# A hybrid decoder layer: the second half of the tokens takes the indexer's first query tile into the keys' loop over contraction tiles

## What is computed

```python
h = rms_norm(x, mix_norm[l])
z = h @ w_in
(aq, ak, av, iq, ik, iw, pin, gu, gv, sq, sk, sv, gl) = jnp.split(z, _split_points(), axis=-1)
...
head_scores = jax.nn.relu(jnp.einsum('bthd,bsd->bths', qib, k_idx_f))
idx_score = jnp.einsum('bth,bths->bts', wb, head_scores)
...
x = x + hybrid_mixer(h, ...)
x = x + swiglu_ffn(rms_norm(x, ffn_norm[l]), ...)
```

## Time and profile before

| | |
|---|---|
| median of 3 runs | 755.93 us (755.53 to 756.05) |
| the profiled execution's own time | 755.91 us |
| its span (what the profile covers) | 754.0 us |
| PE busy | 748.6 us, 99% of the span |
| DVE / ACT / POOL busy | 590.8 / 405.2 / 105.0 us |
| moved by DMA | 89.55 MB |

### The profile page before, as it was taken

One profiled execution on the slowest core, in us unless ns is written; L12 is line 12 of the kernel. 1 busy time (PEld: TensorE's weight loads), 2 busy tenths in 40 slices (PEclk: granted clock), 3 DMA queues, 4 the chain that ended last, 5 costly groups with the idle time before them and its releaser, 6 DMA issues.

```text
span 754.0 us, 11466 instructions
## 1 busy us (share of the span) xinstructions
PE 748.6 (99%) x4494; PEld 660.8 (88%) x4494; DVE 590.8 (78%) x816; ACT 405.2 (54%) x629; POOL 105.0 (14%) x130
## 2 busy tenths in 40 slices
PE   8999999999999999999999999999999999999998
PEld 8988888988888888778888899999889999999886
DVE  5645998878788976425988989889989888888991
ACT  6644545456663654435349655556544556566430
POOL 7100050457303121211231000000000000000000
PEclk9999999999999999999999999999999999999999
DMA  8381213221133222317226725335073333338102
GB/s 274 104 245 42 75 57 113 65 104 57 57 112 99 70 76 92 112 57 278 85 82 176 189 112 157 114 110 210 4 254 108 113 111 111 113 113 321 70 29 83
DMA packets 67877, 89.55 MB, mean 119 GB/s; under 512 B 3108, under 2 KB 52592, under 8 KB 67696
## 3 DMA queue, kind: packets, MB, share of 16 engines
q1 hardware_dynamic: 66224, 85.60, 34.7%
q0 software_dynamic: 1456, 3.09, 2.0%
q10 hardware_dynamic: 144, 0.13, 0.1%
HBM read 81.99 MB, written 4.19 MB: 114 GB/s over the span
## 4 chain that ended last, share of the span: by engine, by line
PE 97%; POOL 1%; issue 1%; DVE 1%; ACT 0%; DVEq 0%; POOLq 0%
PE bank L2358 14%; PE bank L2360 14%; PE bank L2359 14%; PE bank L2784 8%; PE bank L2785 8%; PE bank L2786 8%; PE bank L2846 5%; PE bank L2850 5%; PE bank L2848 5%; PE bank L2725 2%; PE bank L2724 2%; PE bank L2723 2%; PE bank L2755 1%; PE bank L2754 1%; PE bank L2756 1%
## 5 line engine op out<-in xcount | busy, mean ns | idle before, releaser
L2358 PE MATMUL bank<-h_hi,w_hi 128*128 128x512 f32 (+1 forms) x352 | 134.7, 383 | 0.3 <-DVE w_lo L1600 0.3
L2360 PE MATMUL bank<-h_hi,w_lo 128*128 128x512 f32 (+1 forms) x352 | 133.8, 380 | 0.0
L2359 PE MATMUL bank<-h_lo,w_hi 128*128 128x512 f32 (+1 forms) x352 | 133.6, 380 | 0.0
L2784 PE MATMUL bank<-t_hi,w_hi 128*128 128x256 f32 x320 | 88.4, 276 | 0.0
L2786 PE MATMUL bank<-t_hi,w_lo 128*128 128x256 f32 x320 | 88.4, 276 | 0.0
L2785 PE MATMUL bank<-t_lo,w_hi 128*128 128x256 f32 x320 | 88.4, 276 | 0.0
L1529 DVE TENSOR_TENSOR w_lo<-raw,w_hi 128x2048 fp32r<-128x2048 f32 x27 | 64.2, 2379 | 24.1 <-ACT w_hi L918 17.0
L2358 PEld LDWEIGHTS bank<-h_hi,w_hi 128*128 128x128 f32 x352 | 66.2, 188 | 12.7 <-ACT w_hi L981 0.5
L2360 PEld LDWEIGHTS bank<-h_hi,w_lo 128*128 128x128 f32 x352 | 66.2, 188 | 12.6
L2359 PEld LDWEIGHTS bank<-h_lo,w_hi 128*128 128x128 f32 x352 | 66.2, 188 | 12.2
L2785 PE MATMUL bank<-f_lo,w_hi 128*128 128x256 f32 x240 | 66.3, 276 | 0.0
(11 more groups left out here) (374 smaller groups left out, 1858.1 us busy)
## 6 DMA issues: line engine op xcount, KB each, us to landing
raw<-in_w_in_dram SPq DMA_DIRECT2D x26, 1024.0 KB, 5.2
raw<-in_w_ffn_up_dram SPq DMA_DIRECT2D x11, 1024.0 KB, 5.1
raw<-in_w_ffn_gate_dram SPq DMA_DIRECT2D x10, 1024.0 KB, 5.2
raw<-in_w_ffn_down_dram SPq DMA_DIRECT2D x7, 1024.0 KB, 5.1
raw<-in_w_branch_dram SPq DMA_DIRECT2D x4, 1024.0 KB, 4.8
b<-in_w_ffn_down_dram SPq DMA_DIRECT2D x4, 1024.0 KB, 7.0
x_sb<-in_x_dram SPq DMA_DIRECT2D x6, 512.0 KB, 4.7
o<-in_w_out_dram SPq DMA_DIRECT2D x3, 1024.0 KB, 8.5
```

Of the source, the lines that this page charges most:

```text
L2358: mm(dst, l_hi, r_hi, start=start, stop=False)
L2359: mm(dst, l_hi, r_lo, start=False, stop=False)
L2360: return mm(dst, l_lo, r_hi, start=False, stop=stop)
L2784: mm(dst, l_hi, r_hi, start=begin and k == 0, stop=False, skip_group_check=True)
```

## The change

The two or three matmuls of a contraction tile become a helper, `queries(cols, j, k)`. In the second half of the tokens the queries' tile j = 0 is taken into the keys' loop: for each k the two matmuls of the keys are followed by the three of query tile 0. `filled` is still raised in the order keys, j = 0, j = 1. The loop over query tiles behind it starts at j = 1 in the second half. The first half is as before.

```diff
+            def queries(cols, j, k):
+
+                w = slice(w_at(1) + k * CW + j * P, w_at(1) + k * CW + (j + 1) * P)
+                return three(bank[1 + j][:, cols], w_hi[:, w], w_lo[:, w], h_hi[:, k, cols], h_lo[:, k, cols],
+                             k == 0, k == KT - 1)
+
...
                         mm(bank[0][:, cols], w, h_hi[:, k, cols], start=k == 0, stop=False)
                         last = mm(bank[0][:, cols], w, h_lo[:, k, cols], start=False, stop=k == KT - 1)
-                    if half:
-                        last.then_inc(filled, 1)
-                    for j in range(MT):
+                        if half:
+                            if k == KT - 1:
+                                last.then_inc(filled, 1)
+                            last = queries(cols, 0, k)
+                            if k == KT - 1:
+                                last.then_inc(filled, 1)
+                    for j in range(half, MT):
...
-                            w = slice(w_at(1) + k * CW + j * P, w_at(1) + k * CW + (j + 1) * P)
-                            last = three(bank[1 + j][:, cols], w_hi[:, w], w_lo[:, w], h_hi[:, k, cols], h_lo[:, k, cols],
-                                         k == 0, k == KT - 1)
-
+                            last = queries(cols, j, k)
```

## The result

| | before | changed |
|---|---|---|
| median | 755.99 us (755.53 to 756.57, 6 runs) | 758.78 us (757.59 to 759.13, 6 runs) |
| ratio | | 1.003, 95% interval 1.0017 to 1.0044 |
| profiled execution: time, span | 755.91, 754.0 us | 758.81, 756.8 us |
| mean granted clock, by execution | | 0.997 to 0.998 in five, 1.0 in the one of 757.59 |

The change costs 2.79 us, 0.37%, where 0.97 over the median of the three runs shown before was forecast (756.9, range to 757.6). It is slower by more than the interval, and outside the range.

What follows compares the result with a forecast made beforehand. PE, busy 99%, was taken as the bound. The loop's 0.36 us gain is spent waiting for the late `ikw`; chunk 2 starts at 32.20 instead of 31.21, so 755.91 + 0.99 = 756.90 us, range 755.9 to 757.6.

Steps and rivals of the forecast that it cites:

- Part 1: Keys' loop and query tiles on PE: pacing by `h_lo` goes, chunk 1 ends at 29.97, PE 0.36 us ahead.
- a change of bank: Interleaved loop: bank 0 to 1 taken as 0 extra; rival of 0.08 us each, 757.86 us, chance 0.07.
- Part 2: Later transposes for k = 6 and 7: `h_hi` of k = 7 0.64 us late, nothing by themselves.
- Part 3: Later keys' `filled`: ACT's chunk 3 1.72 us late, `ikw` ends 31.77, PE waits 1.37, chunk 2 starts 32.20.
- the DMAs of `iq_lo`: POOL's four DMAs, behind chunk 2: about 1.3 us later, landing by 41.0 before the reader at 43.2, costing nothing.
- Its own wait, `w_lo` of chunk 3, ends at 28.90 + 2.28 = 31.18 and is hidden by that of `ikw`: Start of chunk 2 on PE: its wait for `w_lo` ends at 31.18, hidden by the wait for `ikw`.
- The 0.33 us from L2617 to chunk 2: From the first transposes of `ikw` to chunk 2's first matmul: 0.33 us, so chunk 2 starts at 32.20.
- the gain of 0.36 us: Gain from the keys' loop, expected to be spent waiting for `ikw`; rival that it stays, 755.55 us, chance 0.06.
- the clock: Rival: behind PE's new 1.37 us pause the clock falls to 1.2 GHz; 2 us so spent gives 758.9; chance 0.03.
- The loop, the second place that the prediction named: Clock rival's other place: the interleaved loop, 5.3 us long, falling there would give up to 762 us.
- The passage on cycling through banks: Skill's rule cited against the change: bank cycling with pauses between groups; by it the clock would fall in the loop.

Runs made afterwards that it cites:

- x2: Kernel before, only the keys' `filled` raised later, by the last matmul of k = 5 of query tile 0, second half; 757.54 us.
- x3: Changed kernel with the keys' weights in a place of their own, so `w_hi` of chunk 3 need not wait for `filled`; 756.65 us, ratio 1.001.
- x9: x3 with the query groups of k = 0, 1, 2 all behind the keys of k = 2, transposes at their old moments; 755.93 us, ratio 1.0.
- x5: Changed kernel with 10 filler identity transposes before the wait for `ikw` and 2 behind the transposes of `ikw`; 757.23 us.
- x8: x4 with `iq_lo` of tile 0 ahead of `ikw` on DVE, transposes of `ikw` between chunk 2's first two tiles; 756.29 us, ratio 0.9994.
- x6: Changed kernel with the wait for `ikw` and its four transposes moved from ahead of chunk 2 to between its first two tiles; 759.54 us.
- x4: Kernel before with only the first group of three query matmuls taken ahead of the keys' matmuls of k = 5; 756.01 us, ratio 1.0001.
- x7: Kernel before, only the keys' `filled` raised later, by the last matmul of k = 6 of query tile 0; 759.22 us.
- x1: Changed kernel with 18 filler identity transposes before the wait for `ikw` and 4 behind the transposes of `ikw`; 758.44 us.

## Why the prediction was wrong

**Right.** Part 1: the loop steps at 0.12, ends at 29.98 (forecast 29.97), 0.35 us ahead, and a change of bank costs nothing. Part 2 (the transposes between k = 0 and 1 are those for k = 6, between k = 1 and 2 those for k = 7; no others stand in the loop): `h_hi` of k = 7 at 23.71 (23.69). Part 3: `w_hi` of chunk 3 at 27.00 (26.93), `ikw` ending at 31.84 (31.77), L2624 at 31.89 (31.87). x2, x3 and x9 show each of these causes by itself. Behind chunk 2, the DMAs of `iq_lo` cost nothing that the list of waits shows.

**Wrong, first step: "Its own wait, `w_lo` of chunk 3, ends at 28.90 + 2.28 = 31.18 and is hidden by that of `ikw`".** Chunk 2's first matmul has a second wait, for `taken1`, as the listing ahead of the prediction says in brackets, and DVE raises that at the end of `iq_lo` of tile 0, right behind `ikw`. The 0.33 us from L2617 to chunk 2 was right as the cost of the transposes (0.34 in x5 and x8), but the start of chunk 2 is the end of `iq_lo` plus 0.15 us: 32.58, not 32.20, 0.38 us more (x6 moves the transposes away, and it stays). The interval of 0.35 that the prediction read from before could not show this, since both ends fell nearly together there. For the same reason the gain of 0.36 us could not have reached the end with anything on time (x4, x9). With `taken1` in it the sum is +1.37, 757.3, still inside the range; what the runs with a full clock took is 757.2 to 757.6 (x5, x2, and the 757.59).

**Wrong, second step, and the one that carries the time out of the range: the clock was left out of the sum, at a chance of 0.03.** The mechanism was named, with its place behind the pause. Its price was put at 1 us for each us of work done at 1.2 GHz; 1.84 us of work was done so and cost 1.54 us more in the trace (0.42 us from start to start in place of 0.23). What failed is the reason for leaving it out. "The granted clock stayed 1.00, the 2.4 GHz level, over the stretch with pauses of 0.4 and 0.3 us" says nothing of a pause three times as long. Pauses of 1.16 and 0.28 us brought the clock down in 5 of 6 executions with the change and 4 of 5 in x7, one of 1.85 us in 4 of 5 in x6; pauses of 0.80 and 0.28 us left it at 1.0 in nine of eleven in x2, and what the two others had is open. The loop, the second place that the prediction named, kept its clock: 1.00 throughout, and x5, which cycles alike, kept it to the end. The passage on cycling through banks, which the prediction took from the Trainium skill (TensorE: Matmul & The Clock Gate, "A second HAM failure mode: psum-queue depth-cycling"), speaks of pauses between the groups; this loop has none, and by itself the cycling did nothing here.

So the loss is 1.37 us for the late first `iq_lo` and about 1.5 us for the clock, together the 2.9 between the profiled executions; of the 1.88 us between the forecast and the median, 0.38 is the first step and about 1.5 the second. The later `filled` gives the whole of the first by itself (x2); without it the later transposes would have given 0.61 (x3). The two do not add up, since the longer hides the shorter.

## What to carry to other kernels

When work is put in front of an instruction that raises a semaphore, go through everyone who waits for it, also those who only want a buffer back; then follow their queues until a wait of the bound engine, and read every semaphore of that wait. An interval between two rows tells the cost of its instructions, not that nothing else ends there: before it is carried over, compare its end with the ends on the other engines that its last instruction waits for. And a new pause on TensorE is priced twice, by its length and by what the clock may do behind it, when it is longer than any pause that the trace shows to be harmless.

## What was not expected of the hardware

- A pause of TensorE of 1.16 us between busy stretches, followed by one of 0.28, was enough for the clock to go to 1.2 GHz in most executions, not in all: means of 0.997 or 0.998 in 5 of 6 and 4 of 5, and 1.0 in the others. A single pause of 1.05 us, earlier in x2's profiled execution, left it at 1.00.
- The low level did not come with the pause but behind it, and not at a fixed distance: 1.0 us after PE had gone on with the change (33.59 against 32.58), 0.3 to 0.4 us in x6 and x7 (matmuls slow from their second on, 32.91 against 32.61 and 33.22 against 32.92). It lasted 3.4 us under full work in all three.
- Transposes of the identity into one and the same place of an idle bank kept the clock up in all 16 executions of x1 and x5; 18 of them took 2.18 us, 0.12 each. A pair of transposes of x, with the 0.08 that the matmul behind it takes more, is 0.22, which is about the same.
- Matmuls that alternate between two banks step at 0.12 us, as those that stay in one.
